# Feed-forward layers: one matmul of 512 columns for the upper weights, and the bank's halves added when read

## The reference

```python
D_MODEL = 1024; SEQ = 256; MLP_HIDDEN = 4 * D_MODEL

def squared_relu_mlp(x, w1, w2):
    return jnp.square(jax.nn.relu(x @ w1)) @ w2

for i in range(2):
    xn = rms_norm(h, mix_norm[i])
    y = rwkv7_time_mix(xn, ...) if i == 0 else nsa_mix(xn, ...)
    h = h + y
    h = h + squared_relu_mlp(rms_norm(h, mlp_norm[i]), mlp_w1[i], mlp_w2[i])
return h
```

## Time and profile before

| | |
|---|---|
| median of 3 runs | 805.53 us (801.78 to 820.09) |
| profiled execution, its time | 801.13 us |
| its span | 799.1 us |
| mean granted TensorE clock | 0.970 |
| TensorE busy | 747.2 us, 94% |
| VectorE busy | 524.9 us, 66% |
| ScalarE busy | 375.8 us, 47% |
| DMA | 109.26 MB, mean 137 GB/s |

### The profile page before, as it was taken

The page is one execution under the profiler, slowest core; times in us unless marked ns, Lnnn a source line. Parts: engine busy times, 40 slices in busy tenths (PEclk is TensorE's granted clock), DMA queues, the critical chain, the costliest instruction groups (busy, mean ns, idle before and its releaser), DMA issues.

```text
span 799.1 us, 18237 instructions
## 1 busy us (share of the span) xinstructions
PE 747.2 (94%) x7673; PEld 700.5 (88%) x7673; DVE 524.9 (66%) x745; ACT 375.8 (47%) x577; POOL 72.9 (9%) x50
## 2 busy tenths in 40 slices
PE   7999997797878999999999999987889999999997
PEld 6988987797748999999999979875569999999997
DVE  4896876757544887785555784477846977864541
ACT  6566543221433545454444433437867544444331
POOL 0000005280130000000000010003520000000000
PEclk9999998999987999999999999977999999999999
DMA  9853330000111599867666543330004566676651
GB/s 293 275 172 107 107 106 2 4 3 5 52 54 53 159 244 248 222 197 219 199 187 192 171 139 107 106 105 1 1 2 158 167 202 193 184 225 190 195 171 52
DMA packets 110891, 109.26 MB, mean 137 GB/s; under 512 B 7120, under 2 KB 109776, under 8 KB 110704
## 3 DMA queue, kind: packets, MB, share of 16 engines
q1 hardware_dynamic: 110832, 108.41, 45.5%
HBM read 107.35 MB, written 1.05 MB: 136 GB/s over the span
## 4 chain that ended last, share of the span: by engine, by line
PE 84%; DVE 9%; ACT 4%; issue 1%; POOL 1%; DMA 1%; ACTq 0%; SPq 0%; DVEq 0%; POOLq 0%
PE ps L440 21%; PE ps L441 21%; PE ps L442 21%; PE ps L655 4%; ACT SB L1403 2%; DVE Gs L1640 1%; PE ps L793 1%; PE ps L875 1%; PE ps L554 1%; DVE SB L1952 1%; PE ps L993 1%; DVE nmx L1957 1%; PE ps L1015 1%; ACT PT L1414 1%; DVE LT L1666 1%
## 5 line engine op out<-in xcount | busy, mean ns | idle before, releaser
L1455 DVE TENSOR_TENSOR wlo<-raw,whi 128x1024 fp32r<-128x1024 f32 x188 | 225.4, 1221 | 97.0 <-ACT whi L1070 94.3
L440 PE MATMUL ps<-xh,whi 128*128 128x256 f32 x896 | 251.3, 280 | 1.0 <-ACT R L1143 0.7
L441 PE MATMUL ps<-xl,whi 128*128 128x256 f32 x896 | 248.4, 277 | 0.0
L442 PE MATMUL ps<-xh,wlo 128*128 128x256 f32 x896 | 248.4, 277 | 0.0
L1070 ACT ACTIVATE whi<-raw 128x1024 fp32r<-128x1024 f32 x124 | 130.5, 1059 | 143.4 <-PE ps L442 137.8
L440 PEld LDWEIGHTS ps<-xh,whi 128*128 128x128 f32 x896 | 168.6, 188 | 5.2 <-issue 3.2
L441 PEld LDWEIGHTS ps<-xl,whi 128*128 128x128 f32 x896 | 168.5, 188 | 0.3 <-issue 0.2
L442 PEld LDWEIGHTS ps<-xh,wlo 128*128 128x128 f32 x896 | 168.3, 188 | 0.0
L442 PE MATMUL ps<-hh,wlo 128*128 128x256 f32 x512 | 141.4, 276 | 0.0
L441 PE MATMUL ps<-hl,whi 128*128 128x256 f32 x512 | 141.4, 276 | 0.0
L440 PE MATMUL ps<-hh,whi 128*128 128x256 f32 x512 | 141.4, 276 | 0.0
(11 more groups left out here) (281 smaller groups left out, 998.0 us busy)
## 6 DMA issues: line engine op xcount, KB each, us to landing
raw<-in_mlp_w SPq DMA_DIRECT2D x128, 512.0 KB, 4.5
raw<-in_rwkv_w_in SPq DMA_DIRECT2D x24, 512.0 KB, 5.0
raw<-in_nsa_w_in SPq DMA_DIRECT2D x20, 512.0 KB, 4.5
raw<-in_rwkv_w_out SPq DMA_DIRECT2D x8, 512.0 KB, 3.5
raw<-in_nsa_w_out SPq DMA_DIRECT2D x8, 512.0 KB, 4.0
cw<-in_nsa_cmp_w SPq DMA_DIRECT2D x4, 512.0 KB, 9.3
cst<-in_consts SPq DMA_DIRECT2D x1, 1047.0 KB, 11.2
xtok<-in_x SPq DMA_DIRECT2D x2, 512.0 KB, 4.2
```

Of the source, the lines that this page charges most:

```text
L440: mm(o, wh, hi[:, kk, :], start=(kk == 0), stop=False)
L441: mm(o, wh, lo[:, kk, :], start=False, stop=False)
L442: last = mm(o, wl, hi[:, kk, :], start=False, stop=(kk == ktiles - 1))
L1455: v.tensor_tensor(wlo[:, slot, :], raw[:, slot, :], whi[:, slot, :].bitcast(f32), ALU.subtract)\
```

## The change

In the feed-forward layers the upper and the lower activations become two halves of one tile (xs for the inputs, hs for the hidden values; their addresses are the old ones). A new `unit_mm2` multiplies the upper weights with both in one matmul of 512 columns, which fills a bank: the product with the upper activations in columns 0 to 255, with the lower ones in 256 to 511. The lower weights' matmul of 256 columns goes on accumulating in columns 0 to 255. The halves are added when the bank is read. In the up half ScalarE copies the second half to s2, VectorE adds the first half (rl), then applies relu and ri in SBUF; the square s2 moves from VectorE to ScalarE. In the down half VectorE adds the second half to h and then the first, in two instructions. The projections (linear8) keep `unit_mm`.

```diff
--- before.py
+++ after.py
@@ -136,8 +136,10 @@
     off = lambda n, b=0: blk + n * BLK + b
     misc = blk + 16 * BLK
     A0, B0 = 12, 14
-    xh = [place(f"xh{n}", [P, FT, T], off(12 + 2 * n), r32) for n in range(2)]
-    xl = [place(f"xl{n}", [P, FT, T], off(13 + 2 * n), r32) for n in range(2)]
+
+    xs = [place(f"xs{n}", [P, 2, FT, T], off(12 + 2 * n), r32) for n in range(2)]
+    xh = [x[:, 0, :, :] for x in xs]
+    xl = [x[:, 1, :, :] for x in xs]
 
 
     xtok = place("xtok", [P, TT, D], off(1))
@@ -208,8 +210,8 @@
     yl = place("yl", [P, FT, T], off(10), r32)
 
 
-    hh = place("hh", [P, HT, T], off(0), r32)
-    hl = place("hl", [P, HT, T], off(4), r32)
+    hs = place("hs", [P, 2, HT, T], off(0), r32)
+    hh, hl = hs[:, 0, :, :], hs[:, 1, :, :]
     rl = place("rl", [P, 2, 2, T], off(8))
     s2 = place("s2", [P, 2, 2, T], off(8, 4096))
     sqn = place("sqn", [P, FT, T], off(8))
@@ -440,6 +442,21 @@
                         mm(o, wh, hi[:, kk, :], start=(kk == 0), stop=False)
                         mm(o, wh, lo[:, kk, :], start=False, stop=False)
                         last = mm(o, wl, hi[:, kk, :], start=False, stop=(kk == ktiles - 1))
+                return last
+
+
+
+            def unit_mm2(slot, bank0, kbase, ktiles, both, x=None):
+
+                for k in range(4):
+                    kk = kbase + k
+                    if x and k % 2 == 0:
+                        parts(x, kk // 2)
+                    for m in range(2):
+                        c0 = k * GW + m * P
+                        mm(ps[:, bank0 + m, :], whi[:, slot, c0:c0 + P], both[:, :, kk, :], start=(kk == 0), stop=False)
+                        last = mm(ps[:, bank0 + m, 0:T], wlo[:, slot, c0:c0 + P], both[:, 0, kk, :], start=False,
+                                  stop=(kk == ktiles - 1))
                 return last
 
             def linear8(name, hi, lo, x=None, between=None, groups=4, after_unit=None):
@@ -817,13 +834,13 @@
             pe.wait_ge(sem("yl_last"), 1)
             linear8("o0", yh, yl)
 
-            def mlp_pe(n1, n2, hi, lo, x, i_norm):
+            def mlp_pe(n1, n2, both, x, i_norm):
 
                 for g in range(2):
                     group_free(n1, g)
                     for j in range(2):
                         pe.wait_ge(lo_ready, U0[n1] + 2 * g + j + 1)
-                        unit_mm(2 * g + j, 2 * g, 4 * j, FT, hi, lo, x if g == 0 else None).then_inc(unit_used, 1)
+                        unit_mm2(2 * g + j, 2 * g, 4 * j, FT, both, x if g == 0 else None).then_inc(unit_used, 1)
                     if g == 0:
                         mean_pe(i_norm)
                 with pe.Fori(1, 8) as i:
@@ -831,7 +848,7 @@
                         pe.wait_ge(ev_dve, i * 2 + (EV0[n1] + g - 1))
                         for j in range(2):
                             pe.wait_ge(lo_ready, i * 4 + (U0[n1] + 2 * g + j + 1))
-                            unit_mm(2 * g + j, 2 * g, 4 * j, FT, hi, lo).then_inc(unit_used, 1)
+                            unit_mm2(2 * g + j, 2 * g, 4 * j, FT, both).then_inc(unit_used, 1)
 
                 done = 0 if n1 == "a1" else 16
                 with pe.Fori(0, 2) as i:
@@ -841,9 +858,9 @@
                             if g == 0:
                                 pe.wait_ge(sem("hid_ready"), done + 2 * j + 2)
                             pe.wait_ge(lo_ready, i * 16 + (U0[n2] + 8 * g + j + 1))
-                            unit_mm(j % RING, 2 * g, 4 * j, HT, hh, hl).then_inc(unit_used, 1)
-
-            mlp_pe("a1", "a2", xh[0], xl[0], "a", 1)
+                            unit_mm2(j % RING, 2 * g, 4 * j, HT, hs).then_inc(unit_used, 1)
+
+            mlp_pe("a1", "a2", xs[0], "a", 1)
 
             def between_kc(g):
                 if g == 0:
@@ -1037,7 +1054,7 @@
             weighted(len(items) - 1)
             linear8("o1", xh[1], xl[1], "o1")
 
-            mlp_pe("b1", "b2", xh[0], xl[0], "b", 3)
+            mlp_pe("b1", "b2", xs[0], "b", 3)
 
             for q in range(TT):
                 for k in range(FT):
@@ -1304,19 +1321,30 @@
                     act.wait_ge(unit_used, i * 4 + (u - RING + 1))
                     A(whi[:, 2 * gg + j, :], raw[:, 2 * gg + j, :], ACT.Copy).then_inc(hi_ready, 1)
 
+
+                def lower_half(i, gg):
+                    act.wait_ge(unit_used, i * 4 + (U0[n1] + 2 * gg + 2))
+                    A(s2[:, gg, :, :], ps[:, 2 * gg:2 * gg + 2, T:2 * T], ACT.Copy).then_inc(sem("half_out"), 1)
+
                 def square(i, gg):
-                    act.wait_ge(ev_dve, i * 2 + (EV0[n1] + gg + 1))
+                    act.wait_ge(sem("turned"), i * 2 + (base_ + gg + 1))
                     A(hh[:, ds(i * 4 + 2 * gg, 2), :], rl[:, gg, :, :], ACT.Square).then_inc(sem("hh_ready"), 1)
+                    A(s2[:, gg, :, :], rl[:, gg, :, :], ACT.Square).then_inc(sem("s2_ready"), 1)
 
                 for gg in range(2):
                     split_of(0, gg, 0)
                     if gg == 0:
                         root(i_norm)
+                    if base_:
+                        act.wait_ge(sem("hid_ready"), base_ + gg - 1)
+                    lower_half(0, gg)
                     split_of(0, gg, 1)
                     square(0, gg)
                 with act.Fori(1, 8) as i:
                     for gg in range(2):
                         split_of(i, gg, 0)
+                        act.wait_ge(sem("hid_ready"), i * 2 + (base_ + gg - 1))
+                        lower_half(i, gg)
                         split_of(i, gg, 1)
                         square(i, gg)
                 for g in range(4):
@@ -1775,10 +1803,12 @@
             def mlp_dve(n1, n2, base_, after):
                 def turn(i, gg):
                     dve.wait_ge(unit_used, i * 4 + (U0[n1] + 2 * gg + 2))
-                    v.scalar_tensor_tensor(rl[:, gg, :, :], ps[:, 2 * gg:2 * gg + 2, 0:T], 0.0, normal(2), ALU.max, ALU.mult)\
+                    dve.wait_ge(sem("half_out"), i * 2 + (base_ + gg + 1))
+                    v.tensor_tensor(rl[:, gg, :, :], s2[:, gg, :, :], ps[:, 2 * gg:2 * gg + 2, 0:T], ALU.add)\
                         .then_inc(ev_dve, 1)
                     dve.wait_ge(ev_dve, i * 2 + (EV0[n1] + gg + 1))
-                    v.tensor_tensor(s2[:, gg, :, :], rl[:, gg, :, :], rl[:, gg, :, :], ALU.mult).then_inc(sem("s2_ready"), 1)
+                    v.scalar_tensor_tensor(rl[:, gg, :, :], rl[:, gg, :, :], 0.0, normal(2), ALU.max, ALU.mult)\
+                        .then_inc(sem("turned"), 1)
                     for j in range(2):
                         u = U0[n1] + 2 * gg + j + RING
                         rest(2 * gg + j, i * 4 + (u + 1))
@@ -1800,6 +1830,9 @@
                             add_square(after[0], g - 1)
                     dve.wait_ge(unit_used, U0[n2] + 8 * g + 8)
                     dve.wait_ge(ev_dve, EV0[n2] + g)
+                    part = h[:, 2 * g:2 * g + 2, :]
+                    step(v.tensor_tensor(part, part, ps[:, 2 * (g % 2):2 * (g % 2) + 2, T:2 * T], ALU.add))
+                    settle()
                     add_residual(n2, g)
                     if g < 3:
                         ahead(U0[n2] + 8 * g + 7)
```

## The result

The changed kernel takes 816.33 us (median of 4 runs, 814.67 to 817.96); the kernel before 803.65 in the runs beside it. The ratio is 1.017, 95% interval 1.0121 to 1.0219: slower by 1.7%, where 792.5 us was forecast. All ratios leave out a run more than 1.5% above the fastest of its kernel (820.09 us of the kernel before here, 812.78 us in run 8). The profiled execution took 814.67 us, its span is 812.7, 13.6 above the span before.

The account below looks back on a forecast made before the run. TensorE, busy 94% of the span and throughout the feed-forward halves, was taken as the bound. Span 799.1 - 10.3 + 1.0 + 0.7 = 790.5 us, plus 2.0 outside the span, gave 792.5 us; range 786.5 to 801.

Parts of the forecast that it names:

- part 1: TensorE, feed-forward halves: a wide and narrow pair takes 329.9 ns against 340 for three narrow matmuls, -10.3 us in all.
- the 1.0 of waiting: First layer's up half: TensorE waits for weight remainders behind late loads, +1.0 us (ends 0 and 4.8).
- The bounds for the pair: TensorE, feed-forward halves: savings per pair from 13.4 ns down to nothing, 10.1 taken.
- plain fp32: TensorE: wide matmul at line 591's pace would cost 203 ns more per pair; excluded, fp32r already runs one cycle a column.
- Part 2: Up halves' evacuation: copy, add and moved square cost 0 behind TensorE's time; +1.0 us taken for late weight loads.
- Part 3: Down halves: VectorE's extra add is hidden except in b2's last group, at the kernel's end, +0.7 us.
- kc hidden: After a2's last group: the extra add's 0.73 us fits in the 1.0 in hand before kc's inputs are needed.
- (d): Rival, up halves: the loop of load, split, copy, add, normalise, remainder becomes the bound, +29 us, 820 us; chance 0.05.
- (b): Rival, TensorE: the wide matmul saves nothing, pace proportional to columns or two-piece operand read like two matmuls; 802.8 us; chance 0.1.
- (a): Rival, TensorE: 6.6 ns beyond the columns' time belongs to each matmul, so only -6.8 us; 796.0 us; chance 0.17.
- (c): Rival, TensorE: the narrow matmul also drops to 110 ns and no load is late, -13.7 us; 788.1 us; chance 0.17.
- (e): Rival, TensorE: the wide matmul goes in a narrow one's 113.3 ns, 116 us less, 687 us; chance 0.01.

Follow-up runs that it names:

- run 8: The kernel before, unchanged, run again with a second profile: median 803.56 us of 10 runs, ratio 1.0002.
- run 1: Changed kernel with its 512-column matmul split into two of 256, each with its own weight load; part of the product left out: 809.1 us, ratio 1.0128.
- runs 4 and 9: Changed kernel, matmuls reordered: 4, wide, wide, narrow, narrow per contraction tile, 807.88 us; 9, each unit's eight wide, then its eight narrow, span 810.5 us.

## Why the prediction was wrong

**The step that failed is part 1**, the price of the pair: 216.6 + 113.3 = 329.9 ns was taken, 235 + 118.3 = 353.3 measured. 23.4 ns x 1024 are 24.0 us; less the 1.0 of waiting that didn't come it is 23.0, for the 22.2 from the forecast span (790.5) to the measured one (812.7). The bounds for the pair ran from 326.6 to 340 ns: "nothing saved" was the worst case, because the columns stay the same, and the one row above it, plain fp32, was excluded as too far. Nothing was left in between, where the truth lay.

What was wrong in it, by its own reasoning:
**Part 2 was right**, and its waiting too high: copy, add and the moved square made TensorE wait for nothing, and in run 1's second layer they cost no time. The add came 0.63 us after the copy's start for 0.65 said. ScalarE waited 4.2 us for loads in the two up halves, and TensorE for none; +1.0 was forecast. A pair of groups took 11.3 us for the forecast 10.56, which gave the loads 0.75 more; that this is why no wait came is argued, not shown.

**Part 3 was right**: +0.74 at the end for +0.7, kc hidden.

**The rivals.** In time (d), 820 us, came nearest to the measured 816.33, but by luck: its mechanism, the loop of loads and splits as the bound, would have made TensorE wait in the up halves, and it never did. (b), nothing saved at 802.8, was half right in mechanism: the pace goes by columns. Its price missed that there are two of them. (a), (c) and (e) are out. A slower TensorE had no case among the five, though the sum's unknown was TensorE's price.

**What stays open.** Why there are two paces is not shown, and no rule given here says in every case which of them comes. The wide matmul of the changed kernel and the second narrow one of runs 4 and 9 both follow a narrow one of 118 ns, each with its load begun 116 ns ahead; the first runs at 0.46 ns a column and the second at 0.443. And a stream of narrow matmuls, once at 117.7, kept to it for half of a kernel in runs 1 and 8, yet came back after one matmul in runs 4 and 9. In the slow stream a load has 114 ns from its start to its matmul's, in the other 110, so its weights wait a little each time, which would keep it there, but that is argued and not shown; why runs 4 and 9 come back isn't settled. In run 1 it set in at 280 us, where one matmul took 153 ns to the next instead of 113. That gap alone doesn't do it: the same one stands at 636 us in the second layer, and the pace stayed at 113.

## What to carry to other kernels

Before an operation is made wider to save its overhead, find out which of the overlapped parts sets the pace: shorten one of them by an eighth and see if the pace follows. A price that no row shows can be worse than today's even where the work stays the same; its upper end has to be measured or left in the range. And where a kernel's runs scatter, compare the pace of the same kind of matmul in several places of one execution before calling it noise; here the second pace could be read in the trace of the kernel before.

## What was not expected of the hardware

- An fp32r stream of 128x128 weights and 256 columns has two paces at the same granted clock of 1.00: 113.3 and 117.7 ns a matmul, for the same code in one execution. A layer at the slower one costs about 3.4 us per half; the unchanged kernel had it over a whole layer in one of two profiles, and over parts of its projections in both.
- 512 columns cost 226 to 236 ns, twice the narrow price at one or the other pace, or between: no fixed cost per matmul was saved.
- 224 columns cost 111.7 ns, 256 cost 113.3, and 256 with half the weight columns 119.
- Plain fp32 shows two loads and two matmuls for each matmul of the source: 0.86 us for 512 columns (line 591).
